# A depthwise convolution of 31 taps on TensorE, computed in even and odd tokens with a shared third product

## The reference, cut to what matters

```
def conformer_conv(va, vg, p):            # va, vg: 512 tokens x 1024 channels
    u = va * jax.nn.sigmoid(vg)
    u = depthwise_conv(u, p["conv_w"], p["conv_b"], (15, 15))    # 31 taps, each channel by itself
    return jax.nn.silu(layernorm(u, p["ln_g"], p["ln_b"]))
```

## Time and profile before

| | |
|---|---|
| median of 3 runs | 1636.74 us (1635.92 to 1638.52) |
| the profiled execution: its own time | 1635.73 us |
| its span | 1634.4 us |
| PE busy | 1596.2 us (98%) |
| DVE busy | 983.0 us (60%) |
| ACT busy | 753.4 us (46%) |
| mean granted TensorE clock | 0.993 of full speed |

### The profile page before, as it was taken

One profiled execution on the slowest core, in us unless ns is written; L12 is line 12 of the kernel. 1 busy time (PEld: TensorE's weight loads), 2 busy tenths in 40 slices (PEclk: granted clock), 3 DMA queues, 4 the chain that ended last, 5 costly groups with the idle time before them and its releaser, 6 DMA issues.

```text
span 1634.4 us, 19081 instructions
## 1 busy us (share of the span) xinstructions
PE 1596.2 (98%) x7614; PEld 1268.9 (78%) x7614; DVE 983.0 (60%) x1413; ACT 753.4 (46%) x1050; POOL 23.7 (1%) x44
## 2 busy tenths in 40 slices
PE   5999999999999999999999999999999999999998
PEld 2888767677788888888888777777888888888886
DVE  5877778787886566545765644455456544444223
ACT  5788665755544333333355564344334333333212
POOL 0000000000000000000000000000000000000000
PEclk9999999999999999999999999999999999999999
DMA  9344566563233332333212222222323323233321
GB/s 382 136 147 168 153 194 193 191 191 128 93 100 103 103 93 88 103 104 100 93 54 89 78 65 65 78 65 69 99 90 103 103 91 103 90 96 98 103 90 52
DMA packets 54104, 185.75 MB, mean 114 GB/s; under 512 B 7392, under 2 KB 7392, under 8 KB 53120
## 3 DMA queue, kind: packets, MB, share of 16 engines
q1 hardware_dynamic: 47472, 152.70, 29.0%
q0 software_dynamic: 5104, 18.72, 3.7%
q10 hardware_dynamic: 1440, 13.11, 1.9%
HBM read 173.91 MB, written 2.10 MB: 108 GB/s over the span
## 4 chain that ended last, share of the span: by engine, by line
PE 89%; DVE 6%; ACT 3%; issue 1%; DMA 0%; DVEq 0%; ACTq 0%; POOLq 0%
PE banks L1783 24%; PE banks L1785 24%; PE banks L1784 24%; PE banks L1918 3%; PE banks L2286 2%; PE banks L2288 2%; PE banks L2287 2%; DVE w_lo L1014 1%; PE banks L2128 1%; ACT w_hi L473 1%; PE banks L2142 1%; PE banks L2176 0%; DVE n_t L1143 0%; DMA vec<-vecs 0%; PE banks L2082 0%
## 5 line engine op out<-in xcount | busy, mean ns | idle before, releaser
L1783 PE MATMUL banks<-h_hi,w_hi 128*128 128x512 f32 x1344 | 530.6, 395 | 7.6 <-DVE M L1552 3.2
L1785 PE MATMUL banks<-h_hi,w_lo 128*128 128x512 f32 x1344 | 525.2, 391 | 0.0
L1784 PE MATMUL banks<-h_lo,w_hi 128*128 128x512 f32 x1344 | 525.1, 391 | 0.0
L1014 DVE TENSOR_TENSOR w_lo<-raw,w_hi 128x1024 fp32r<-128x1024 f32 (+1 forms) x274 | 324.9, 1192 | 254.6 <-ACT w_hi L473 254.0
L473 ACT ACTIVATE w_hi<-raw 128x1024 fp32r<-128x1024 f32 (+1 forms) x274 | 280.2, 1026 | 161.0 <-PE banks L2288 76.9
L1783 PEld LDWEIGHTS banks<-h_hi,w_hi 128*128 128x128 f32 x1344 | 253.5, 189 | 70.6 <-issue 8.6
L1785 PEld LDWEIGHTS banks<-h_hi,w_lo 128*128 128x128 f32 x1344 | 253.4, 189 | 53.6
L1784 PEld LDWEIGHTS banks<-h_lo,w_hi 128*128 128x128 f32 x1344 | 253.6, 189 | 51.8 <-issue 0.5
L1783 PE MATMUL banks<-y_hi,w_hi 128*128 128x512 f32 x192 | 75.7, 394 | 0.0
L1784 PE MATMUL banks<-y_lo,w_hi 128*128 128x512 f32 x192 | 74.7, 389 | 0.0
L1785 PE MATMUL banks<-y_hi,w_lo 128*128 128x512 f32 x192 | 74.7, 389 | 0.0
(11 more groups left out here) (408 smaller groups left out, 2236.6 us busy)
## 6 DMA issues: line engine op xcount, KB each, us to landing
raw<-weights SPq DMA_DIRECT2D x263, 512.0 KB, 3.5
mraw<-modt POOLq DMA_DIRECT2D x32, 512.0 KB, 4.2
mod<-modr ACTq DMA_DIRECT2D x4, 2048.0 KB, 22.5
rep<-U SPq DMA_DIRECT2D x96, 64.9 KB, 2.4
raw<-weights SPq DMA_DIRECT2D x16, 256.0 KB, 3.7
rep<-U SPq DMA_DIRECT2D x32, 64.8 KB, 2.0
X<-x_in ACTq DMA_DIRECT2D x2, 1024.0 KB, 6.7
out<-Xt SPq DMA_DIRECT2D x8, 256.0 KB, 2.0
```

The lines of the kernel that those rows point to most:

```text
L1014: tt(slot(w_lo, c, 0, w), slot(raw, c, 0, w), slot(w_hi, c, 0, w).bitcast(F32), ALU.subtract).then_inc(S["lo"], 1)
L1783: mm(o, wh, r_hi, start=start, stop=False)
L1784: mm(o, wh, r_lo, start=False, stop=False)
L1785: return mm(o, wl, r_hi, start=False, stop=stop)
```

## The change

The signal `U` is now stored split by token parity: a tile has its even tokens first (`HW` = 271 columns with the padding) and then the odd ones. Call these halves a and b, b' the half b shifted by one, and w0, w1 the taps of even and odd index. The even outputs w0\*b + w1\*a are computed as (w0 + w1)\*a + w0\*(b - a), the odd outputs w0\*a + w1\*b' as (w0 + w1)\*a + w1\*(b' - a): three products of 16 taps over 256 tokens each (a star is a convolution). The two on differences go into the halves of bank 3, the common one into half of bank 2, and DVE adds it to both.

```
-            e.wait_ge(S["uu"], i + 1)
-            if i > 1:
-                e.wait_ge(S["mm"], C["cw", i - 2] + 1)
+            e.wait_ge(S["cin"], 2 * i + 1)
+            if i:
+                e.wait_ge(S["mm"], C["cw", i - 1] + 1)
+            n = TH + 3
             for j in range(4):
                 for s in range(4):
-                    n = T + 7 if s < 3 else T + 6
-                    e.dma_start(rep[i % 2][32 * s:32 * s + 32, j * RW:j * RW + n],
-                                U[32 * j:32 * j + 32, (i + 1) * UW + 8 * s:(i + 1) * UW + 8 * s + n]).then_inc(s_rep[i % 2], 16)
+                    dst = rep[32 * s:32 * s + 32, 3 * RW * j:3 * RW * (j + 1)].rearrange("p (q w) -> p q w", w=RW)[:, :, 0:n]
+                    src = U[32 * j:32 * j + 32, (i + 1) * UW:(i + 2) * UW].rearrange("p (q w) -> p q w", w=HW)[:, :, 4 * s:4 * s + n]
+                    e.dma_start(dst[:, 0:2, :], src).then_inc(s_rep, 16)
+                    e.dma_start(dst[:, 2, :], odd_d[32 * j:32 * j + 32, 4 * s:4 * s + n]).then_inc(s_rep, 16)
...
# ACT, convolved(i)
-            fn(tile(U, i, T, UW), bank(3), ACT.Identity, bias=cb2[:, i:i + 1]).then_inc(S["cpe"], 1)
+            if i:
+                e.wait_ge(S["csum"], i)
+            fn(both[:, :], bank(2, TH), ACT.Identity, bias=cb2[:, i:i + 1]).then_inc(S["cpe"], 1)
...
# DVE
+        def differences(i):
+            even, odd = U[:, (i + 1) * UW:(i + 1) * UW + HW], U[:, (i + 1) * UW + HW:(i + 2) * UW]
+            if i:
+                e.wait_ge(s_rep, 512 * i)
+            own.did(tt(odd_d[:, :], U[:, (i + 1) * UW + HW + 1:(i + 2) * UW + 1], even, ALU.subtract))
+            own.wait()
+            tt(odd, odd, even, ALU.subtract).then_inc(S["cin"], 1)
+        def tap_sums(i):
+            c = C["cw", i]
+            e.wait_ge(s_raw[c % RING], 16 * (c // RING + 1))
+            if i:
+                e.wait_ge(S["mm"], C["cw", i - 1] + 1)
+            tt(tap_sum[:, :], slot(raw, c, 0, T), slot(raw, c, T, T), ALU.add).then_inc(S["cin"], 1)
         def convolved(i):
             e.wait_ge(S["cpe"], i + 1)
-            if i:
-                e.wait_ge(S["csum"], i)
+            own.did(tt(by_parity(tile(U, i, T, UW)), bank(3).rearrange("p (two t) -> p two t", two=2),
+                       both[:, :].rearrange("p (a t) -> p a t", a=1).to_broadcast([P, 2, TH]), ALU.add))
+            own.wait()
             tt(csum[:, :], csum[:, :], tile(U, i, T, UW), ALU.add).then_inc(S["csum"], 1)
...
-            if i:
+            if i == 0:
+                e.wait_ge(S["uu"], 1)
+                differences(0)
+            else:
                 convolved(i - 1)
...
             stt(tile(sga, i), tile(sga, i), 1.0, bank(2), ALU.add, ALU.mult).then_inc(S["sga"], 1)
+            tap_sums(i)
...
             stt(u[:, :], u[:, :], 0.5, tg[:, :], ALU.mult, ALU.mult).then_inc(S["yact"], 1)
-            if i == NT - 1:
+            if i < NT - 1:
+                differences(i + 1)
+            else:
                 convolved(i)
...
# PE
             c = ready("ga", i)
             if i:
                 e.wait_ge(S["sga"], i)
+                e.wait_ge(S["cpe"], i)
             blocks(bank(2), c, h_hi, h_lo).then_inc(S["mm"], 1)
...
-            e.wait_ge(s_rep[i % 2], 256 * (i // 2 + 1))
+            e.wait_ge(s_rep, 512 * (i + 1))
             if i:
-                e.wait_ge(S["cpe"], i)
-            for step in range(8):
-                for j in range(4):
-                    a = j * RW + step
-                    last = mm(banks[32 * j:32 * j + 32, 3 * 512:4 * 512], slot(raw, c, (8 * j + step) * 32, 32), rep[i % 2][:, a:a + T],
-                              start=step == 0, stop=step == 7)
+                e.wait_ge(S["csum"], i)
+            for q, o in ((1, 3 * 512), (2, 3 * 512 + TH), (0, 2 * 512)):
+                if q == 0:
+                    e.wait_ge(S["cin"], 2 * i + 2)
+                    e.wait_ge(S["sga"], i + 1)
+                for step in range(4):
+                    for j in range(4):
+                        a, w = (3 * j + q) * RW + step, (4 * j + step) * 32
+                        taps = tap_sum[:, w:w + 32] if q == 0 else slot(raw, c, (q - 1) * T + w, 32)
+                        last = mm(banks[32 * j:32 * j + 32, o:o + TH], taps, rep[:, a:a + TH], start=step == 0, stop=step == 3)
```

More of the change, by code:

```diff
@@ L22 @@
 EPS = 1e-6
-RW = T + 8
+TH = T // 2
+HW = UW // 2
+RW = TH + 4
 FFN_TILES = 22
@@ L132 @@
     "norm_t norm_hi norm_lo xp conv uhi ulo gread e2 mv sq thr scan sig uu "
-    "tgt sgb sgat sga cpe csum yact ybhi yblo ymu usum usq yln ysil yga yhi yalo res xsq xsum "
+    "tgt sgb sgat sga cin cpe csum yact ybhi yblo ymu usum usq yln ysil yga yhi yalo res xsq xsum "
     "lpad lcp dhi dsub dlo gsil gy gyhi gylo osq osum rbs "
@@ L228, in program @@
     s_mod0 = [ctx.enter_context(nc.semaphore(f"s_mod0_{j}")) for j in range(4)]
-    s_rep = [ctx.enter_context(nc.semaphore(f"s_rep{s}")) for s in range(2)]
+    s_rep = ctx.enter_context(nc.semaphore("s_rep"))
     s_mraw = [ctx.enter_context(nc.semaphore(f"s_mraw{s}")) for s in range(MOD_RING)]
@@ L248, in program @@
     p = Plan(area)
-    U = p("U", (NT + 1) * UW)
+    U = p("U", (NT + 1) * UW + 16)
     o_sga = p.at = (p.at + 255) // 256 * 256
@@ L256, in program @@
     mraw = p("mraw", MOD_RING * CW)
-    rep = [p(f"rep{k}", 4 * RW) for k in range(2)]
+    rep = p("rep", 4 * 3 * RW)
+    odd_d, tap_sum, both = p("odd_d", HW), p("tap_sum", T), p("both", TH)
     csum = p("csum", T)
@@ L294, in program @@
     place = {qk: n for n, qk in enumerate(first)}
-    u3 = U[:, :].rearrange("p (f w) -> p f w", w=UW)
+    u3 = U[:, 0:(NT + 1) * UW].rearrange("p (f w) -> p f w", w=UW)
     s1, s2, sqa, sqb = (at(f"s_{n}", T, limit // 32 * 32 - 2 * K * (n + 1)) for n in range(4))
@@ L388, in mod_slot, with by_parity, split_tokens @@
         return mraw[:, s + o:s + o + w]
+    def by_parity(t):
+        return t.rearrange("p (t two) -> p two t", two=2)
+    def split_tokens(t):
+        return t.rearrange("p (two w) -> p two w", two=2)[:, :, 0:TH]
     def pooled_rows(t):
@@ L1213, in dve @@
         e.wait_ge(S["norm_lo"], 2 * NT)
-        own.did(e.memset(u3[:, :, 0:HALO], 0.0))
-        own.did(e.memset(u3[:, :, HALO + T:UW], 0.0))
+        own.did(e.memset(u3[:, :, 0:HALO // 2], 0.0))
+        own.did(e.memset(u3[:, :, HALO // 2 + TH:HW + HALO // 2 + 1], 0.0))
+        own.did(e.memset(u3[:, :, HW + HALO // 2 + 1 + TH:UW], 0.0))
+        own.did(e.memset(U[:, (NT + 1) * UW:], 0.0))
         own.did(e.memset(ctx_state, 0.0))
         own.did(e.memset(csum[:, :], 0.0))
-        for k in range(2):
-            own.did(e.memset(rep[k][96:128, :].rearrange("p (j w) -> p j w", w=RW)[:, :, T + 6:T + 7], 0.0))
         own.wait()
@@ L1225, in dve @@
             product("va", i)
-            stt(tile(U, i, T, UW, UW + HALO), tg[:, :], 1.0, bank(0), ALU.add, ALU.mult).then_inc(S["uu"], 1)
+            stt(split_tokens(U[:, (i + 1) * UW + HALO // 2:(i + 1) * UW + HALO // 2 + 2 * HW + 2]), by_parity(tg[:, :]), 1.0,
+                by_parity(bank(0)), ALU.add, ALU.mult).then_inc(S["uu"], 1)
             if i < NT - 1:
@@ L2359, in lay_out @@
     cw = a["ev_conv_w"][0]
-    taps = np.zeros((NT, 4, 32, 4, 8, 32), np.float32)
+    taps = np.zeros((NT, 4, 32, 2, 4, 4, 32), np.float32)
     for n in range(CONV_K):
         for q in range(32):
-            taps[:, n // 8, q, :, n % 8, q] = cw[n].reshape(NT, 4, 32)[:, :, q]
+            taps[:, n // 8, q, n % 2, :, n // 2 % 4, q] = cw[n].reshape(NT, 4, 32)[:, :, q]
     taps = taps.reshape(NT, P, CW)
```

## The result

| | before | changed |
|---|---|---|
| median | 1636.63 us (4 runs) | 1799.56 us (1798.06 to 1801.36, 4 runs) |
| ratio | | 1.0991, 95% interval 1.0978 to 1.1005 |
| span of the profiled execution | 1634.4 us | 1798.1 us |
| mean granted TensorE clock | 0.993 | 0.953 |

A forecast was written before the change was run, and what follows sets the result against it. TensorE alone was taken to bound the kernel before. Rounds of 45.9 us put the end 158.9 us later; with 0.4 and 3 for the clock, 162 over the span of 1634.4 led to a median of 1799 us, range 1745 to 1880.

The forecast's parts named there:

- 32 issues: SP's copy issues of one round, each taken at 0.632 us: 20.2 us.
- last issue to gates: From the round's last copy issue through the load of `gb` and ACT's `w_hi` copy to `head_gates`: 8.9 us.
- gates to recurrence output: From the start of `head_gates` on ACT through the scans to `yact` on DVE: 15.8 us.
- differences: DVE's two subtractions of 271 columns behind `yact`, which the next copies wait for: 1.0 us (0.9 to 1.4).
- period: One round of the loop, from SP's issue to its next issue: 45.9 us in place of 26.3.
- sum over features starts: TensorE's sum behind the output products: at 550.8 instead of 391.87 us, plus about 0.4 for `yb_lo`.
- The ring: Chain without TensorE: SP issue, loads, ACT, gates, scans, `yact`, differences, next issue; 45.9 us a round, chance 0.80.
- The 3 us for a slow clock behind the last round: TensorE's output work after the last convolution starts at a lower clock after idling: 3 us (0 to 5).
- Twice the price for two runs: Upper bound on SP's queue: each issue costs 1.18 us, 37.8 a round; milder high end 0.9 each.
- a price by rows: Rival: SP's issue time follows descriptor rows, 512 to 1536 a set: 30.1 us, total 1878; chance 0.10.
- The second ring, through bank 2: Rival: issues cheap or hidden, but `ga` waits for `cpe` from ACT: 30.5 us a round, total 1665; chance 0.06.
- The rival of a gain: All waits are absorbed and the convolution's saved quarter counts in full on TensorE: 1623 us; chance 0.03.

The follow-up runs named there:

- after: The changed kernel itself, as first measured against the kernel before: 1799.56 us, ratio 1.0991.
- all four edits: Changed kernel with early differences, 16 three-run copies, ACT's early copy of the common product, and round 0's differences in the loop before: 1631.4 us, ratio 0.9961.

## Why the prediction was right

Taken by its own steps, with the round from 320 to 366 us:

| step | forecast | profile after |
|---|---|---|
| 32 issues | 20.2 us at 0.632 | 20.9 at 0.628 and 0.594 plus gaps |
| last issue to gates | 8.9 | 8.4 (load of `gb` landed in 5.8, not 6.3) |
| gates to recurrence output | 15.8 | 15.8 (349.42 to 365.21) |
| differences | 1.0 | 0.8 |
| period | 45.9 | 46.0 |
| last convolution ends | 536.4 us | 538.4 us |
| sum over features starts, against 391.87 | +159.3 and 3 for the clock | 553.37: +161.5 |

- **The ring is shown, link by link.** Moving the differences, halving the issues and moving the loads ahead each took 71 to 82 us off, and each touches only one link; leaving out three quarters of the convolution's matmuls, or taking away TensorE's wait for the common product, took nothing off.
- **One term was wrong and hidden by others.** The 3 us for a slow clock behind the last round did not occur in this profile (granted clock 1.00 from 538.4 to 554; the stretch took 15.0 us instead of 14.4). The rounds were 46.2 us in the mean and not 45.9, 2.0 us over seven; the first convolution ended at 215.1, where the prediction's terms put it. That the sum came within 1 us of the median is luck in this part. (The convolution before, 7.08 us in the prediction, is 7.10 in the earlier trace rows; nothing hangs on it.) Of the 163.7 us of span, 161.5 lie ahead of the sum over features; where the last 2.2 arose was not looked into, and runs differ by as much.
- **The bounds were wide because the price of an issue was not in the trace for the new shapes.** The value of the nearest row (0.63) held (0.628 and 0.594). Twice the price for two runs, and a price by rows, were both wrong.
- **The second ring, through bank 2, was named but priced too low.** Its 30.5 us a round were worked out at full clock; two runs in which TensorE waits on the path came out 2 to 3 us a round above such a sum (early differences with three-run copies 32.7 against 30.0, halved copies of the kernel before 33.9 against 31.9), and in the rounds shown the lower clock behind the wait makes 2.8 and 1.7 us of it. In the forecast itself this did no harm, since TensorE was off the path.
- **The rival of a gain** needed three separate waits and the start of round 0 changed. With all four edits the gain is 6 us of the 14 that the matmuls save.

## What to carry to other kernels

Count DMA issues, not bytes: where a queue pays 0.6 us for each small copy, a change that doubles their number must be checked against what stands behind them in that queue. When a wait is added, follow what is queued behind the waiter until either an engine with slack ends the path or it returns to where it started; a ring's period is the sum of its links, whatever each engine's busy share is. And a wait listed in the profile is a loss only if its removal shortens the ring: test it before believing its microseconds.

## What the runs showed of the hardware

- An SBUF to SBUF copy of 32 partitions held the issuing queue for 0.59 to 0.63 us at the median, with one, two or three runs a partition and 32 to 97 KB; 512 KB from memory on 128 partitions held it for 0.33 to 0.46 us, and up to 0.58 in after.
- GpSimd's tap sums and differences on SBUF slowed DVE beside them: 3.53 instead of 2.35 us for two operations, while GpSimd took twice DVE's time for a tap sum.
- Behind 5.4 us without a matmul in a round of 32 the granted clock was 0.50 (1.2 GHz) for the next 5 us, and 0.74 over the 11 us of `ga` and `gx`; behind 4.3 us it was 0.81 over the convolution of the kernel before with halved copies.
